# Feed-forward steps 3 to 10 with the gate and up products turned, and the down products placed one step sooner

## The chip, the cores and the metric

One core of one Trainium2 chip runs the whole kernel as a single launch. The metric is device time in microseconds (us). PE is the matrix engine (TensorE), PEld its weight loads, DVE the vector engine, ACT the scalar engine, POOL is GpSimd, SP the engine that issues the loads of weights.

## The reference

256 rows of width 1024 pass four transformer layers and then two layers of another kind. The change lies in the feed-forward part that closes each of the four:

```
def swiglu(x, w_gate_up, w_down):
    g, u = jnp.split(x @ w_gate_up, 2, axis=-1)
    return (jax.nn.silu(g) * u) @ w_down          # D_FF = 2816
x = layer_norm(ALPHA * x + swiglu(x, w_gate_up[i], w_down[i]), ln2_g[i], ln2_b[i])
```

The second kind of layer is conditioned by twelve rows of 512 values, `silu(c) @ w_ada + b_ada`. They depend on nothing else, and the kernel makes them in the midst of the feed-forward parts.

## The kernel before, in words

**Precision.** All is fp32. For a product the kernel splits each operand in a high part, rounded to the matrix engine's fp32r, and a low part, the rest, and adds three products: high by high, high by low, low by high. A tile of weights (128x2048, 1 MB) is loaded to one of three buffers `w_raw` (SP, line 2465), rounded to `w_high` by ACT (`high`, line 1528), and subtracted to `w_low` by DVE (`low`, line 1777). Five places hold high and low parts (`RING`). The loads of tile t wait until the low part of tile t-3 is made.

**Feed-forward.** `Plan.feed_forward` goes through 11 steps of 256 columns. A step has two tiles of `w_gate_up` (each half of the 1024 rows of the contraction, with 256 gate and 256 up columns) and one tile of `w_down`. I call the up tiles of step s sA and sB and its down tile Ds. Each tile is used by two jobs (`gemm`), one for each block of 128 rows of x (rb 0 and 1), each of 12 products of 512 columns. The rows' turned x (`xt_high`, `xt_low`) is the stationary operand, the weights move (line 1309). The result for 128 rows, gate in one half of a PSUM bank and up in the other, is read by ACT (`gate`: silu to SBUF, line 1663) and DVE (`gate`: times up, line 2128). Since the down product needs h with the hidden columns on the partitions, PE turns h of each step by four transposes (`turn_h`, line 1422), ACT copies them out as `ht_high` (line 1672), and DVE makes `ht_low` (line 2134). The down job (line 1268) has 12 products of 512 columns too and adds into PSUM banks kept for the whole layer. Steps 0 and 1 are made together, 3 to 9 are: up jobs A0, A1, B0, B1 of step s, a conditioning row if one is due, turn of h(s-1), then the two down jobs of D(s-3). Step 10 has no down. The tail does D7, D8, D9, D10 for rb 0, then for rb 1, with the turn of h(10) after D8.

**Conditioning rows.** After steps 3 to 8 a tile of `w_ada` is put in the stream (`ada_tile`). DVE multiplies and adds it (`ada_sum`, four instructions, line 1800) instead of splitting it. After every second tile the sum is split (lines 1679 and 2145), and two products by a matrix of ones (lines 1429, 1430) add over partitions. DVE adds the row to `ada_rows` (line 2154).

**Order.** Each engine runs the same list of steps, in order, and waits only on semaphores. When a tile has been used by both its jobs it is given back; `split()`, called after each job through `on()`, first emits the `low` of what was rounded at the split before, then, if a tile is owed, the next `high`, and only then counts what this job gave back. So tile n+5 is rounded one job after tile n was given back, and its low part is queued one job after that. Tiles are given back in order only: a tile used once holds back those behind it.

```
 def split(self):
     self.low()
     if self.owed:
         self.owed -= 1
         self.high()
     self.owed, self.given_back = self.owed + self.given_back, 0
```

**PSUM.** Banks 0 and 1 are the ring `gemms`, 6 and 7 the ring `tr` (for turns and conditioning rows). A use of a ring waits until the use two before it is released.

Of the kernel before, what the change touches and what calls it, by code (L numbers as in the profile page):

```python
# [50 lines left out]
RING = 5  # L51
PIECES = (4, 2)
N_TILES = (3 * KINDS.count("A") + len(KINDS) * (2 * (5 + 1 + 2) + 3 * FF_STEPS) + DEPTH_2 * 2 * (6 + 8 + 2))
BOTH = ("turned", "memory", "tail", "queries")
BESIDE = MEMW + IDX_H + HD
PAIRS = ((1, 2), (3, 0))
BIG = -1.0e30
# [93 lines left out]
class Plan:  # L151
# [127 lines left out]
    def block_turned(self, name, layer, cols, gen, then, begin=None):  # L279


        uses = [self.gemms.take() for _ in range(2)]
        for half in range(2):
            t = self.tile(name, layer, cols, "half", 4 * half)
            for n in range(2):
                self.gemm(t, n, half, gen, "gemm", uses[n], "turned")
                if half:
                    then(n, uses[n], t)
                if begin and half and n:
                    begin()  # L290
                self.on()

    def group(self, blocks, gen, after, prompt=False, more=None):
# [254 lines left out]
    def feed_forward(self, layer):  # L548

        gen, out = ("ff", layer), ("ln2", layer)  # L550
        acc = [self.wide.take() for _ in range(RB)]

        def gate(step):
            def then(rb, use, tile):
                self.up_use[layer, step, rb] = use
                self.add("gate", Ff(layer, step, rb, use, tile))
            return then

        def turn(step):
            self.ff_turn[layer, step] = self.tr.take()  # L560
            self.add("turn_h", (layer, step))

        def down(step, t, rb, prompt=False, part=None):
            self.gemm(t, rb, step, ("h", layer), "wide", acc[rb], "down", prompt, part)

        def down_tile(step):
            t = self.down_tile[layer, step] = self.tile("w_down", layer, step, "down", 0)
            return t

        def late():  # L570
            self.xt(gen, 1)
        self.group([("w_gate_up", layer, step, "up", gate(step)) for step in range(2)], gen,
                   [[self.split, self.split, late, self.split], [self.split] * 4])
        turn(0)
        for step in range(2, FF_STEPS):
            if step == 2:
                self.add("ada_ones", layer)
            self.block("w_gate_up", layer, step, gen, gate(step), "up")
            self.ada_row()
            if step == 2 and layer == LAST:  # L580
                self.add("load_modulation", 0)
            if step == 3 and layer in (1, LAST):
                self.add("norm_rows", layer // 2)
            if step == 9 and layer in (1, LAST):
                self.add("modulation", layer // 2)
            turn(step - 1)
            if step < FF_STEPS - 1:
                if step > 2:
                    t = down_tile(step - 3)
                    for rb in range(RB):  # L590
                        down(step - 3, t, rb)
                        self.on()
                if 2 < step < 9:
                    self.ada_tile()
        steps = range(FF_STEPS - 4, FF_STEPS)
# [576 lines left out]
def by_rows(j):  # L1172

    return j.kind == "dil"
# [37 lines left out]
def tensor_program(pe, K):  # L1212
# [29 lines left out]
    def idle(count):  # L1242

        pe.wait_ge(*K.zeroed.at(0))
        for _ in range(count):
            e.matmul(psum[:, K.wide.place(0), :], K.zeros[:, 0:P], K.zeros[:, :], start=True, stop=True)

    def gemm(j):
        s, rb = plan.place[j.tile] % RING, j.rb
        hi, lo = K.w_hi[:, s, :], K.w_lo[:, s, :]  # L1250
        if j.kind == "down":
            first, last = j.half == 0, j.half == FF_STEPS - 1
            if first:
# [3 lines left out]
            for n, h in passes:  # L1257
                if n == 0:
                    pe.wait_ge(*K.high.at(j.tile))
                    pe.wait_ge(*K.ht_high.at((j.gen[1], j.half)))  # L1260
                elif n == 1:
                    pe.wait_ge(*K.tr.out(plan.ff_turn[j.gen[1], j.half]))
# [243 lines left out]
def scalar_program(act, K):  # L1506
# [159 lines left out]
    def turn_h(j):  # L1666
        layer, step = j
        use = plan.ff_turn[j]
        if step > 3:
# [65 lines left out]
    def final_halves(_):  # L1735
# [6 lines left out]

    pieces = {"first_piece": first_piece, "high": high, "xt": xt, "rope_tables": rope_tables, "constants": constants, "evac": evac, "evac_ki": evac_ki,
              "turn": turn, "dots": dots, "exps": exps, "recip": recip, "turn_prob": turn_prob, "weigh": weigh, "mix_split": mix_split,
              "gate": gate, "turn_h": turn_h, "ada_halves": ada_halves, "rms": rms, "ret_weigh": ret_weigh, "sb_scores": sb_scores,
              "sb_halves": sb_halves, "sb_later": sb_later, "sb_split": sb_split, "final": final,
              "final_halves": final_halves}
    for what, job in plan.steps:
# [5 lines left out]
def vector_program(v, K):  # L1754
# [376 lines left out]
    def turn_h(j):  # L2131
# [2 lines left out]
        e.tensor_tensor(K.ht_lo[at], psum[:, K.tr.place(use), :].rearrange("p (c s) -> p c s", s=SEQ),  # L2134
                        K.ht_hi[at].bitcast(F32), ALU.subtract).then_inc(K.tr.sem(use), 1)

    def ada_ones(layer):
# [157 lines left out]
    def final(rb):  # L2297
# [9 lines left out]
              "turn_h": turn_h, "ada_ones": ada_ones, "ada_halves": ada_halves, "ada": ada, "modulation": modulation, "norm_rows": norm_rows, "rms": rms,  # L2307
# [166 lines left out]
class Kernel:  # L2474


    def __init__(self, nc, ctx, T, out):
# [16 lines left out]
        self.xt_hi = sb("xt_high", [P, KC, SEQ], F32R)  # L2494
        self.xt_lo = sb("xt_low", [P, KC, SEQ], F32R)
# [41 lines left out]
        self.ff_silu = [t.rearrange("p (r c) -> p r c", r=RB) for t in ff[0:2]]  # L2537
        self.ff_h = [t.rearrange("p (r c) -> p r c", r=RB) for t in ff[2:4]]
        self.ada_acc = ff[12:14]
        self.prob = [work[:, 1024 * n:1024 * n + 1024] for n in range(2)]  # L2540
        self.probt = [work[:, 2048 + 1024 * n:3072 + 1024 * n] for n in range(2)]
        self.idx = work[:, 2048:2048 + RB * 704].rearrange("p (r c) -> p r c", r=RB)
# [87 lines left out]
        self.silu_done, self.ht_high = signal("silu_done"), signal("ht_high")  # L2630
# [240 lines left out]
```

## Time and profile before

| | us |
|---|---|
| median of 3 runs (1553.69 to 1554.85) | 1554.36 |
| the profiled execution, its own time | 1553.68 |
| its span, first to last instruction | 1551.9 |
| PE busy | 1528.5 (98%) |
| DVE busy | 1088.2 (70%) |
| ACT busy | 760.7 (49%) |

The profiled execution took 1.8 us more than its span and 0.7 us less than the median. Busy times are sums over a whole engine; what one edit is worth is read in the stretch that it touches, from the starts of neighbouring instructions. In a row of the timeline "x4" is four instructions in a row, and the duration reaches from the start of the first to the end of the last; products overlap at their ends, so the pace is the distance between starts.

### The profile page before, as it was taken

The page shows a single profiled execution, that of the slowest core. Times are in us where ns is not written, and L with a number is a line of the kernel's source. Part 1 is how long each engine was busy: PE and PEld are TensorE (multiplying, and loading weights), DVE is VectorE, ACT ScalarE, POOL GpSimd, SP SyncE. Part 2 cuts the span into 40 slices and gives each one's busy share as a digit, 9 for nine tenths or more (in the row PEclk, how much of TensorE's full clock was granted, in tenths as well). Part 3 has the DMA queues.
Part 4 walks back from the last instruction along what each step waited for, and adds up shares of the span by engine and source line. Part 5 has one row for each costly group of instructions (what it writes and reads, how often), then busy time and mean ns, then how long its engine had stood idle before and what let it go on. Part 6 is the DMA issues. An engine that isn't in the chain of part 4 may idle for free.

```text
span 1551.9 us, 19840 instructions
## 1 busy us (share of the span) xinstructions
PE 1528.5 (98%) x8091; PEld 1267.8 (82%) x8091; DVE 1088.2 (70%) x1561; ACT 760.7 (49%) x963; POOL 52.1 (3%) x89
## 2 busy tenths in 40 slices
PE   9999999999999999999999999999999999999997
PEld 7887788888878888888788888877888888978986
DVE  6986866656777775676966756888667678567764
ACT  5657444444445443346544343566444434574463
POOL 1100000000000000000000000000100000000010
PEclk9999999999999999999999999999999999999999
DMA  8661666644435766352476654533766645433530
GB/s 320 245 231 55 226 224 264 249 174 179 163 104 201 262 261 243 138 215 83 178 252 234 244 225 148 204 109 136 267 257 236 223 166 223 164 118 140 217 122 27
DMA packets 45898, 299.87 MB, mean 193 GB/s; under 512 B 5540, under 2 KB 5796, under 8 KB 12528
## 3 DMA queue, kind: packets, MB, share of 16 engines
q1 hardware_dynamic: 39600, 278.74, 48.6%
q0 software_dynamic: 5776, 19.01, 3.7%
q8 instruction: 64, 1.05, 0.3%
q10 hardware_dynamic: 432, 0.85, 0.1%
q14 instruction: 26, 0.21, 0.0%
HBM read 296.20 MB, written 2.65 MB: 193 GB/s over the span
## 4 chain that ended last, share of the span: by engine, by line
PE 83%; DVE 9%; ACT 4%; issue 2%; DMA 0%; POOL 0%; POOLq 0%; SPq 0%; DVEq 0%; ACTq 0%
PE psum L1309 53%; PE psum L1268 15%; PE psum L1303 7%; DVE w_low L1777 3%; PE psum L1163 2%; PE psum L1238 1%; PE psum L1422 1%; ACT work L1604 1%; PE psum L1325 1%; ACT w_high L1528 1%; PE psum L1306 1%; DVE work L2061 1%; PE psum L1376 1%; DVE work L2099 1%; DVE xt_low L1811 0%
## 5 line engine op out<-in xcount | busy, mean ns | idle before, releaser
L1528 ACT ACTIVATE w_high<-w_raw 128x2048 fp32r<-128x2048 f32 (+1 forms) x240 | 456.4, 1903 | 230.7 <-DMA w_raw<-in_weights 144.9
L1777 DVE TENSOR_TENSOR w_low<-w_raw,w_high 128x2048 fp32r<-128x2048 f32 (+2 forms) x240 | 530.0, 2214 | 34.4 <-ACT w_high L1528 33.3
L1309 PE MATMUL psum<-w_high,xt_high 128*128 128x512 f32 (+1 forms) x1376 | 378.6, 395 | 1.4 <-DVE x_rows L1875 0.7
L1309 PE MATMUL psum<-w_high,xt_low 128*128 128x512 f32 (+1 forms) x1376 | 368.4, 388 | 0.3 <-DVE xt_low L1811 0.3
L1309 PE MATMUL psum<-w_low,xt_high 128*128 128x512 f32 (+1 forms) x1376 | 368.1, 388 | 0.0
L1309 PEld LDWEIGHTS psum<-w_high,xt_low 128*128 128x128 f32 x1376 | 257.4, 188 | 54.8 <-DVE xt_low L1811 0.7
L1309 PEld LDWEIGHTS psum<-w_low,xt_high 128*128 128x128 f32 x1376 | 257.3, 188 | 53.7 <-DVE w_low L1777 0.4
L1309 PEld LDWEIGHTS psum<-w_high,xt_high 128*128 128x128 f32 x1376 | 249.8, 188 | 52.5 <-DVE x_rows L1875 2.3
L2128 DVE TENSOR_TENSOR arena<-arena,psum 128x256 f32<-128x256 f32 x88 | 36.9, 420 | 205.4 <-ACT arena L1663 205.0
L1663 ACT ACTIVATE arena<-psum 128x256 f32<-128x256 f32 x88 | 33.7, 383 | 218.5 <-PE psum L1309 218.5
L1268 PE MATMUL psum<-w_high,ht_high 128*128 128x512 f32 x352 | 99.9, 401 | 0.0
L1268 PE MATMUL psum<-w_high,ht_low 128*128 128x512 f32 x352 | 96.1, 390 | 0.0
L1268 PE MATMUL psum<-w_low,ht_high 128*128 128x512 f32 x352 | 95.9, 390 | 0.0
L1268 PEld LDWEIGHTS psum<-w_high,ht_low 128*128 128x128 f32 x352 | 66.1, 188 | 14.4
L1268 PEld LDWEIGHTS psum<-w_low,ht_high 128*128 128x128 f32 x352 | 66.1, 188 | 14.1
L1268 PEld LDWEIGHTS psum<-w_high,ht_high 128*128 128x128 f32 x352 | 63.2, 188 | 11.0
L1560 ACT ACTIVATE arena<-psum 128x512 f32<-128x512 f32 (+1 forms) x54 | 30.4, 569 | 83.0 <-PE psum L1309 46.3
L1800 DVE SCALAR_TENSOR_TENSOR arena<-w_raw,c_col,arena 128x512 f32<-128x512 f32 x84 | 62.9, 749 | 2.6
L2364 POOL TENSOR_TENSOR norm_rstd<-norm_rstd,half_neg 128x1 f32<-128x1 f32 (+1 forms) x32 | 22.8, 715 | 1126.8 <-DVE norm_rstd L1860 871.2
L1604 ACT ACTIVATE work<-work,neg_max 128x128 f32<-128x128 f32 (+3 forms) x80 | 38.0, 477 | 28.2 <-DVE neg_max L2061 27.9
L1920 DVE TENSOR_SCALAR arena<-psum 128x512 f32<-128x512 f32 x25 | 17.2, 688 | 48.3 <-PE psum L1309 25.4
L1811 DVE TENSOR_TENSOR xt_low<-psum,xt_high 128x512 fp32r<-128x512 f32 (+1 forms) x48 | 31.0, 672 | 18.0 <-ACT xt_high L1537 17.5
(253 smaller groups left out, 1494.8 us busy)
## 6 DMA issues: line engine op xcount, KB each, us to landing
w_raw<-in_weights SPq DMA_DIRECT2D x260, 1024.0 KB, 4.8
norm_params<-in_ln_g POOLq DMA_DIRECT2D x8, 512.0 KB, 4.4
norm_params<-in_ln_b POOLq DMA_DIRECT2D x8, 512.0 KB, 5.9
w_raw<-in_weights SPq DMA_DIRECT2D x4, 656.0 KB, 6.1
kv_outside<-arena POOLq DMA_DIRECT2D x3, 512.0 KB, 4.5
mem_kv<-kv_outside POOLq DMA_DIRECT2D x3, 512.0 KB, 3.7
norm_params<-mods_outside POOLq DMA_DIRECT2D x3, 512.0 KB, 5.8
x_rows<-in_x SPq DMA_DIRECT2D x4, 256.0 KB, 5.6
```

Of the source, the lines that this page charges most:

```text
L1163: m = e.matmul(pieces[n][1], left, right, start=banks[i] not in banks[:i], stop=banks[i] not in banks[i + 1:])
L1268: m = e.matmul(psum[:, K.wide.place(j.use) + h, :], left[:, c, rb * P:rb * P + P], right[:, w:w + BLK], start=first and c == 0 and n == 0, ...
L1303: m = e.matmul(dst, right[:, c + b * P:c + b * P + P], rows[:, kk, :], start=first and b == 0, stop=last and b == 1)
L1309: m = e.matmul(psum[:, bank, 0:w], rows[:, kk, rb * P:rb * P + P], right[:, at:at + w], start=first, stop=last)
L1528: e.activation(K.w_hi[:, g % RING, 0:w], K.w_raw[:, r, 0:w], ACT.Copy).then_inc(K.high.hit(t), 1)
L1560: m = e.activation(to, out, ACT.Silu if j.silu else ACT.Copy, scale=K.evac_scale(j.where, j.rb))
L1604: m = e.activation(pr, pr, ACT.Exp, bias=K.negmax[:, slot, n:n + 1], scale=-1.0, accum_out=K.expsum[:, slot, n:n + 1])
L1663: e.activation(K.ff_silu[j.step % 2][:, j.rb, :], psum[:, K.gemms.place(j.use), 0:FF_STEP], ACT.Silu).then_inc(K.silu_done.hit((j.layer, j ...
L1777: m = e.tensor_tensor(K.w_lo[:, s, 0:n], K.w_raw[:, r, 0:n], K.w_hi[:, s, 0:n].bitcast(F32), ALU.subtract)
L1800: m = e.scalar_tensor_tensor(out=acc, in0=w, scalar=c, in1=acc, op0=ALU.mult, op1=ALU.add)
L1811: m = e.tensor_tensor(lo[at], psum[:, K.tr.place(j.use), 0:n * P].rearrange("p (c s) -> p c s", s=P), hi[at].bitcast(F32), ALU.subtract)
L2128: e.tensor_tensor(K.ff_h[j.step % 2][:, j.rb, :], K.ff_silu[j.step % 2][:, j.rb, :], bank[:, FF_STEP:BLK], ALU.mult).then_inc(K.gemms.sem( ...
```

## The change

- From step 3 (`BY_ROWS`) on, up jobs are made the other way about (`block_up`, `gemm_up`). The weights are stationary, 128 columns at a time, and the rows' high and low parts, laid out as one buffer `xt_both`, move together. A job n takes the columns n*128 to n*128+127 of gate and of up: eight products of 512 columns (256 rows by high part, 256 by low) and eight of 256 columns with the low weights. h comes out with the hidden columns on the partitions. Job 0 takes both banks of `gemms`, job 1 both of `tr`.
- The half of each bank that holds weights by the rows' low parts is copied out by ACT (`gate_turned`, 128x512) and added to the other half by DVE, gate and up apart. Then come ACT's silu and DVE's product. The wait for ACT's silu stands behind the DVE's first addition.
- The transposes of `turn_h` go for steps 3 to 10. `split_h` on ACT and DVE makes `ht_high` and `ht_low` from SBUF. Steps 0 to 2 keep theirs.
- Down jobs move: step s has D(s-2) and not D(s-3), beginning with D0 in step 2. Step 8 has D6 for rb 0 alone, step 9 D6 for rb 1 alone, step 10 none, and the tail is as it was, with `split_h` of step 10 after D8. The turn of h(2) stands between the two jobs of D0.
- The conditioning row stands after a down job and not ahead of the turn. The `modulation` of step 9 follows the down job.

```
@@ Plan @@
+    def block_up(self, layer, step, gen):
+        uses = [(ring.take(), ring.take()) for ring in (self.gemms, self.tr)]
+        for half in range(2):
+            t = self.tile("w_gate_up", layer, step, "up", 4 * half)
+            for n in range(2):
+                self.gemm(t, n, half, gen, ("gemm", "turn")[n], uses[n], "up")
+                if half:
+                    self.add("gate_turned", Up(layer, step, n, uses[n], t))
+                self.on()
@@ feed_forward @@
         def turn(step):
-            self.ff_turn[layer, step] = self.tr.take()
-            self.add("turn_h", (layer, step))
+            if step < BY_ROWS:
+                self.ff_turn[layer, step] = self.tr.take()
+                self.add("turn_h", (layer, step))
+            else:
+                self.add("split_h", (layer, step))
...
-            self.block("w_gate_up", layer, step, gen, gate(step), "up")
-            self.ada_row()
+                self.block("w_gate_up", layer, step, gen, gate(step), "up")
+            else:
+                self.block_up(layer, step, gen)
...
-            turn(step - 1)
-            if step < FF_STEPS - 1:
-                if step > 2:
-                    t = down_tile(step - 3)
-                    for rb in range(RB):
-                        down(step - 3, t, rb)
-                        self.on()
-                if 2 < step < 9:
-                    self.ada_tile()
+            if step != BY_ROWS:
+                turn(step - 1)
+            if step == FF_STEPS - 1:
+                break
+            if step < FF_STEPS - 2:
+                t = down_tile(step - 2)
+            for rb in range(RB) if step < FF_STEPS - 3 else (step - FF_STEPS + 3,):
+                down(min(step - 2, FF_STEPS - 5), t, rb)
+                self.on()
+                self.ada_row()
+                if rb == 0 and step == BY_ROWS - 1:
+                    turn(step)
...
+            if 2 < step < 9:
+                self.ada_tile()
@@ tensor_program @@
+    def gemm_up(j, hi, lo):
...
+        work = [(4 * j.half + k, b, k * BLK + b * FF_STEP + j.rb * P) for k in range(4) for b in range(2)]
+        pe.wait_ge(*K.high.at(j.tile))
+        for kk, b, c in work:
+            e.matmul(banks[b].rearrange("p (n s) -> p n s", n=2), hi[:, c:c + P], K.xt_both[:, :, kk, :], start=kk == 0, stop=False)
+        pe.wait_ge(*K.taken.at(j.tile))
+        for kk, b, c in work:
+            m = e.matmul(banks[b][:, 0:SEQ], lo[:, c:c + P], K.xt_both[:, 0, kk, :], start=False, stop=kk == KC - 1)
@@ scalar_program @@
+    def gate_turned(j):
...
+        e.activation(K.ff_rest[j.n], psum[:, first:first + 2, SEQ:BLK], ACT.Copy).then_inc(K.rest_out.hit((j.layer, j.step, j.n)), 1)
+        act.wait_ge(*ring.out(j.uses[0]))
+        e.activation(K.ff_silu[j.step % 2][:, j.n, :], K.ff_gate(j), ACT.Silu).then_inc(K.silu_done.hit((j.layer, j.step, j.n)), 1)
@@ vector_program @@
+    def gate_turned(j):
...
+        for use, row in zip(j.uses, (K.ff_gate(j), K.ff_up(j))):
+            e.tensor_tensor(row, psum[:, ring.place(use), 0:SEQ], row, ALU.add).then_inc(ring.sem(use), 1)
...
+        e.tensor_tensor(K.ff_h[j.step % 2][:, j.n, :], K.ff_silu[j.step % 2][:, j.n, :], K.ff_up(j),
+                        ALU.mult).then_inc(K.h_made.hit((j.layer, j.step, j.n)), 1)
+    def split_h(j):
...
+        v.wait_ge(*K.ht_high.at(j))
+        e.tensor_tensor(K.ht_lo[at], K.ff_h[j[1] % 2], K.ht_hi[at].bitcast(F32),
+                        ALU.subtract).then_inc(K.ht_low.hit(j), 1)
```

## Rows read from the trace of the kernel before

**Rows 1.** The page, parts 1 and 2: busy us, share, instructions; granted clock in tenths

```profile
PE 1528.5 (98%) x8091; PEld 1267.8 (82%) x8091; DVE 1088.2 (70%) x1561; ACT 760.7 (49%) x963; POOL 52.1 (3%) x89
...
PEclk9999999999999999999999999999999999999999
```

**Rows 2.** The waits of PE: us in total, times, longest us

```profile
PE psum L1376 <- ACT arena L1648: 2.3, 3, 1.2
...
PE psum L1238 <- DVE arena L2117: 1.7, 1, 1.7
```

**Rows 3.** Busy time by stretch, a step without a conditioning row and one with

```profile
230.23:247.05 16.82, 16.82 (x78) 13.90 (x76) 11.13 (x12) 7.42 (x7) 0.00 (x0) 1.00 0.67 251
247.05:264.29 17.24, 17.24 (x79) 14.28 (x78) 11.95 (x12) 6.90 (x6) 0.00 (x0) 1.00 0.68 255
```

**Rows 4.** The timeline of the second of these: start us, duration us, instruction

```profile
252.49 1.07 PE L1309 MATMUL psum<-w_high,xt_high 128*128 128x512 f32 x4
...
255.21 1.07 PE L1309 MATMUL psum<-w_high,xt_high 128*128 128x512 f32 x4
...
257.93 0.39 PE L1429 MATMUL psum<-ada_high,ones 128*128 128x512 f32 x1
...
258.38 0.60 PE L1422 MATMUL psum<-ident,arena 128*128 128x128 f32 x4
...
258.88 2.28 DVE L1777 TENSOR_TENSOR w_low<-w_raw,w_high 128x2048 fp32r<-128x2048 f32 x1
...
262.35 3.09 DVE L1800 SCALAR_TENSOR_TENSOR arena<-w_raw,c_col,arena 128x512 f32<-128x512 f32 x4
...
264.29 1.07 PE L1309 MATMUL psum<-w_high,xt_high 128*128 128x512 f32 x4
...
265.85 1.92 ACT L1528 ACTIVATE w_high<-w_raw 128x2048 fp32r<-128x2048 f32 x1 [4.42 <-DMA w_raw<-in_weights]
```

**Rows 5.** The timeline of a stretch of products of 256 columns

```profile
1331.62 1.12 PE L1303 MATMUL psum<-xt_high,w_high 128*128 128x256 f32 x8
1332.58 1.12 PE L1303 MATMUL psum<-xt_low,w_high 128*128 128x256 f32 x8
```

**Rows 6.** The timeline of steps 9, 10 and the tail of layer 0

```profile
332.67 1.92 ACT L1528 ACTIVATE w_high<-w_raw 128x2048 fp32r<-128x2048 f32 x1 [3.13 <-PE psum L1268]
...
341.05 1.91 ACT L1528 ACTIVATE w_high<-w_raw 128x2048 fp32r<-128x2048 f32 x1
...
343.30 0.60 PE L1422 MATMUL psum<-ident,arena 128*128 128x128 f32 x4
343.50 0.38 ACT L1663 ACTIVATE arena<-psum 128x256 f32<-128x256 f32 x1 [0.53 <-PE psum L1309]
343.65 1.18 PE L1268 MATMUL psum<-w_high,ht_high 128*128 128x512 f32 x4
343.92 0.42 DVE L2128 TENSOR_TENSOR arena<-arena,psum 128x256 f32<-128x256 f32 x1 [2.30 <-ACT arena L1663]
343.93 0.60 ACT L1672 ACTIVATE ht_high<-psum 128x512 fp32r<-128x512 f32 x1
344.25 2.29 DVE L1777 TENSOR_TENSOR w_low<-w_raw,w_high 128x2048 fp32r<-128x2048 f32 x1
344.43 1.91 ACT L1528 ACTIVATE w_high<-w_raw 128x2048 fp32r<-128x2048 f32 x1
...
346.45 0.68 DVE L2134 TENSOR_TENSOR ht_low<-psum,ht_high 128x512 fp32r<-128x512 f32 x1
...
347.06 2.28 DVE L1777 TENSOR_TENSOR w_low<-w_raw,w_high 128x2048 fp32r<-128x2048 f32 x1
```

**Rows 7.** DMA issues of the weights: KB each, us to landing

```profile
w_raw<-in_weights SPq DMA_DIRECT2D x260, 1024.0 KB, 4.8
```

**Rows 8.** The page, part 5: the weight loads of the down products, mean ns

```profile
L1268 PEld LDWEIGHTS psum<-w_high,ht_low 128*128 128x128 f32 x352 | 66.1, 188 | 14.4
```

**Rows 9.** The timeline of PE at the kernel's start, products on zeros

```profile
1.19 3.17 PE L1246 MATMUL psum<-arena 128*128 128x512 bf16 x7 [1.19 <-DVE arena L1757]
```

More of the change, by code:

```diff
@@ L39 @@
 FF_STEPS = D_FF // FF_STEP
+BY_ROWS = 3
 ALPHA = float((2 * len(KINDS)) ** 0.25)
@@ L53 @@
 N_TILES = (3 * KINDS.count("A") + len(KINDS) * (2 * (5 + 1 + 2) + 3 * FF_STEPS) + DEPTH_2 * 2 * (6 + 8 + 2))
-BOTH = ("turned", "memory", "tail", "queries")
+BOTH = ("turned", "memory", "tail", "queries", "up")
 BESIDE = MEMW + IDX_H + HD
@@ L145 @@
 Ff = namedtuple("Ff", "layer step rb use tile")
+Up = namedtuple("Up", "layer step n uses tile")
 Ada = namedtuple("Ada", "row use")
@@ L1246, in idle @@
             e.matmul(psum[:, K.wide.place(0), :], K.zeros[:, 0:P], K.zeros[:, :], start=True, stop=True)
+    def gemm_up(j, hi, lo):
+        ring = (K.gemms, K.tr)[j.rb]
+        if j.half == 0:
+            for use in j.use:
+                pe.wait_ge(*ring.free(use))
+        banks = [psum[:, ring.place(use), :] for use in j.use]
+        for r in range(RB):
+            use = plan.xt_uses[j.gen, r, j.half]
+            pe.wait_ge(*K.xt_high.at(use))
+            pe.wait_ge(*K.tr.out(use))
+        work = [(4 * j.half + k, b, k * BLK + b * FF_STEP + j.rb * P) for k in range(4) for b in range(2)]
[5 more added lines that the diff above has]
+            m = e.matmul(banks[b][:, 0:SEQ], lo[:, c:c + P], K.xt_both[:, 0, kk, :], start=False, stop=kk == KC - 1)
+        m.then_inc(K.multiplied.hit((j.tile, j.rb)), 1)
     def gemm(j):
@@ L1250, in gemm @@
         hi, lo = K.w_hi[:, s, :], K.w_lo[:, s, :]
+        if j.kind == "up":
+            gemm_up(j, hi, lo)
+            return
         if j.kind == "down":
@@ L1261, in gemm @@
                 elif n == 1:
-                    pe.wait_ge(*K.tr.out(plan.ff_turn[j.gen[1], j.half]))
+                    pe.wait_ge(*(K.tr.out(plan.ff_turn[j.gen[1], j.half]) if j.half < BY_ROWS
+                                 else K.ht_low.at((j.gen[1], j.half))))
                 else:
@@ L1673, in turn_h @@
                      ACT.Copy).then_inc(K.ht_high.hit(j), 1)
+    def gate_turned(j):
+        ring = (K.gemms, K.tr)[j.n]
+        first = min(ring.place(use) for use in j.uses)
+        act.wait_ge(*K.multiplied.at((j.tile, j.n)))
+        if j.step > BY_ROWS:
+            act.wait_ge(*K.h_made.at((j.layer, j.step - 1, j.n)))
+        e.activation(K.ff_rest[j.n], psum[:, first:first + 2, SEQ:BLK], ACT.Copy).then_inc(K.rest_out.hit((j.layer, j.step, j.n)), 1)
+        act.wait_ge(*ring.out(j.uses[0]))
+        e.activation(K.ff_silu[j.step % 2][:, j.n, :], K.ff_gate(j), ACT.Silu).then_inc(K.silu_done.hit((j.layer, j.step, j.n)), 1)
+    def split_h(j):
+        layer, step = j
+        if step > 3:
+            act.wait_ge(*K.multiplied.at((plan.down_tile[layer, step - 4], 1)))
+        for n in range(2):
+            act.wait_ge(*K.h_made.at((layer, step, n)))
+        e.activation(K.ht_hi[step % 4], K.ff_h[step % 2], ACT.Copy).then_inc(K.ht_high.hit(j), 1)
     def ada_halves(row):
@@ L1744, in scalar_program @@
               "turn": turn, "dots": dots, "exps": exps, "recip": recip, "turn_prob": turn_prob, "weigh": weigh, "mix_split": mix_split,
-              "gate": gate, "turn_h": turn_h, "ada_halves": ada_halves, "rms": rms, "ret_weigh": ret_weigh, "sb_scores": sb_scores,
+              "gate": gate, "turn_h": turn_h, "gate_turned": gate_turned, "split_h": split_h, "ada_halves": ada_halves, "rms": rms, "ret_weigh": ret_weigh, "sb_scores": sb_scores,
               "sb_halves": sb_halves, "sb_later": sb_later, "sb_split": sb_split, "final": final,
@@ L2135, in turn_h, with split_h @@
                         K.ht_hi[at].bitcast(F32), ALU.subtract).then_inc(K.tr.sem(use), 1)
+    def gate_turned(j):
+        ring = (K.gemms, K.tr)[j.n]
+        v.wait_ge(*K.rest_out.at((j.layer, j.step, j.n)))
+        for use, row in zip(j.uses, (K.ff_gate(j), K.ff_up(j))):
+            e.tensor_tensor(row, psum[:, ring.place(use), 0:SEQ], row, ALU.add).then_inc(ring.sem(use), 1)
+        if j.step - 2 < BY_ROWS:
+            v.wait_ge(*K.turned.at(plan.ff_turn[j.layer, j.step - 2]))
+        else:
+            v.wait_ge(*K.ht_low.at((j.layer, j.step - 2)))
+        v.wait_ge(*ring.out(j.uses[1]))
+        v.wait_ge(*K.silu_done.at((j.layer, j.step, j.n)))
+        e.tensor_tensor(K.ff_h[j.step % 2][:, j.n, :], K.ff_silu[j.step % 2][:, j.n, :], K.ff_up(j),
+                        ALU.mult).then_inc(K.h_made.hit((j.layer, j.step, j.n)), 1)
+    def split_h(j):
+        at = j[1] % 4
+        v.wait_ge(*K.ht_high.at(j))
+        e.tensor_tensor(K.ht_lo[at], K.ff_h[j[1] % 2], K.ht_hi[at].bitcast(F32),
+                        ALU.subtract).then_inc(K.ht_low.hit(j), 1)
     def ada_ones(layer):
@@ L2306, in vector_program @@
               "choose": choose, "scores": scores, "recip": recip, "turn_prob": turn_prob, "weigh": weigh, "mix_split": mix_split, "gate": gate,
-              "turn_h": turn_h, "ada_ones": ada_ones, "ada_halves": ada_halves, "ada": ada, "modulation": modulation, "norm_rows": norm_rows, "rms": rms,
+              "turn_h": turn_h, "gate_turned": gate_turned, "split_h": split_h, "ada_ones": ada_ones, "ada_halves": ada_halves, "ada": ada, "modulation": modulation, "norm_rows": norm_rows, "rms": rms,
               "modulate": modulate, "rotate": rotate, "ret_scores": ret_scores, "ret_norm": ret_norm,
@@ L2493, in __init__ @@
         self.w_lo = sb("w_low", [P, RING, TW], F32R)
-        self.xt_hi = sb("xt_high", [P, KC, SEQ], F32R)
-        self.xt_lo = sb("xt_low", [P, KC, SEQ], F32R)
+        self.xt_both = sb("xt_both", [P, 2, KC, SEQ], F32R)
+        self.xt_hi, self.xt_lo = self.xt_both[:, 0, :, :], self.xt_both[:, 1, :, :]
         self.x = sb("x_rows", [P, RB, D])
@@ L2539, in __init__ @@
         self.ada_acc = ff[12:14]
+        self.ff_rest = [work[:, BLK * n:BLK * n + BLK].rearrange("p (b s) -> p b s", b=2) for n in range(2)]
         self.prob = [work[:, 1024 * n:1024 * n + 1024] for n in range(2)]
@@ L2735, in group_on_scalar, with ff_gate, ff_up @@
         return 0 if by_rows(j) and self.unit_pieces(j) > 4 else None
+    def ff_gate(self, j):
+        places = [(self.gemms, self.tr)[j.n].place(use) for use in j.uses]
+        return self.ff_rest[j.n][:, int(places[0] > places[1]), :]
+    def ff_up(self, j):
+        places = [(self.gemms, self.tr)[j.n].place(use) for use in j.uses]
+        return self.ff_rest[j.n][:, int(places[0] < places[1]), :]
     def unit_pieces(self, j):
```

3 lines of the change are left out of this document (2 added, 1 removed).

## The prediction

> **What bounds the kernel now.** I read the page first: PE is busy 98% of the span, DVE 70%, ACT 49%, at the full granted clock in all slices [rows 1]. So what counts is PE's own instructions, and any new wait of PE. PE's waits come next: the largest group is 2.3 us in all, the longest single one 1.7 us, and no line of the feed-forward (L1309 up, L1268 down, L1422 turn) has one worth naming [rows 2]. The stretches confirm it: a step of 16.82 us and one of 17.24 us are PE busy from end to end, with DVE busy 11.13 and 11.95 us and ACT 7.42 and 6.90 us [rows 3]. The timeline gives the parts. Three groups of four products start 2.72 us apart for a job of 12: 0.2267 us for one of 512 columns [rows 4]. The conditioning row takes 257.93 to 258.38, 0.45 us; from there to the next step's first product are 5.91 us, of which two down jobs are 24 x 0.2267 = 5.44, so the turn of h costs PE 0.47 us [rows 4]. The step of rows 3 without a row gives 16.82 - 72 x 0.2267 = 0.50. I take 0.48.
>
> **Removed.** 8 turns x 4 layers = 32 x 0.48 = 15.4 us, all on PE, which sets the time.
>
> **Added on PE.** A job has now 8 products of 512 and 8 of 256 columns: the same 6144 columns, four instructions more. 256 columns go at 0.96 / 8 = 0.120 us [rows 5]. The job is 8 x 0.2267 + 8 x 0.120 = 2.77 us against 2.72, and 128 jobs (4 x 8 x 4) cost 128 x 0.053 = +6.8 us. Those 256-column rows have weights as the moving side; the pace should hang on columns alone. That the 512 columns now come from two places 256 apart in xt_both has no row: I take nothing, bounded by nothing and by the pace of two products of 256 (0.240 for 0.227, 1024 products: +13.7 us), and lean to nothing, since both ends are runs of 256 neighbours. Solved for two widths, rows 4 and 5 give 0.0133 us per product beyond 2.4 GHz streaming.
> The Trainium skill (TensorE: Matmul & The Clock Gate, "Wait — 56ns, not 53.3ns?") has only about 2.5 ns per warm product on top of N/2.4 GHz. By that this term would be 512 x 2.5 ns = 1.3 us and not 6.8. The trace's 13 ns disagrees, and it decides.
>
> **Added on ACT and DVE, hidden in steps 3 to 9.** Per step: ACT two copies of 128x512 (0.60 each) more, DVE four additions of 128x256 for the banks (starts 0.33 apart, 343.92 to 344.25) [rows 6] and the wait for silu. I walk a step with a row from t = 0, the end of B0; queue starts from rows 6: PE end to ACT 0.20, ACT end to DVE 0.04, silu to the next 0.28, a low part 2.20 to the next, a subtraction of 512 0.61.
> - Job 0: copy 0.20-0.80, additions 0.84 and 1.17, silu 1.31, product 1.73-2.06. ACT then rounds a tile 1.59-3.50.
> - Job 1 (PE ends 2.77): copy 3.5-4.1, additions 4.15 and 4.5, product 5.1-5.4. Then on DVE low 5.4-7.6, split of h 8.2, ada_sum (3.09 [rows 4]) 11.3, row or its split 12.0, low 14.2, low 16.4. The next step's first addition is due at 17.0 + 0.84 = 17.8: 1.4 us to spare.
> - PE's conditioning row wants job 1's first bank at 5.49, it is free at 4.6: 0.9 us to spare. The next up jobs want the banks 8.2 us after their last product.
> - The loads: ACT already sits 4.42 us before 265.85 for a tile that waits for the low part of 258.88 [rows 4]. That low part comes 1.7 us later, so the rounding ends near 14.2 instead of 12.6, still 3 us ahead of the next copy of B0.
> Price: 0. Where a spare falls under zero, PE waits once a step (rival 2).
> The moves in steps 2 to 9 cost nothing either: D(s-2) reads a split of h one step old; the turn of h(2) has a down job of 2.72 us over the gate chain, 0.6 us now (343.30 to 343.92 and on). SP's loads keep their number and only change order; POOL gets no new instruction.
>
> **Added in the tail.** This is the term that decides. D6 is used once in step 8 and once after step 9, and tiles come back in order. So 9A and 9B wait behind it, nothing is rounded in step 9, and D7, D8, D9, D10 are rounded in the four jobs of step 10, the next layer's first tile N in the job after. In the kernel before D9 starts at 332.67 on the end of D6, D10 at 341.05, N at 344.43, and N's low part at 347.06 lies ahead of the tail's second job [rows 6]. Now, from t = 0 at the end of 10B0 (D7 and D8 rounded by then, D7 low too; D8's low is queued behind job 0's DVE work):
> - DVE: additions 0.84, 1.17; product 1.73; low D8 2.06-4.35; job 1's additions 4.26, 4.59 (its copy ran 3.4-4.0 behind the rounding of D9), product 5.15, low D9 5.48, split of h(9) 7.68, low D10 8.29-10.5.
> - N's load waits for low D8, is issued at 4.35 and lands 4.8 us later [rows 7], 9.15. ACT rounds N 9.15-11.06 and then, behind it, copies h(10) 11.1-11.7. DVE: low N 11.1, split of h(10) 13.3-13.98.
> - PE: 10B1 ends 2.77, D7, D8, D9 at 10.93. D10 wants the high part of h(10) at 10.93 and gets it at 11.7; after two products, 0.45, its pass by the low part was due at 11.38, but stands till 14.0.
> So D10 of rb 0 ends 2.6 us late. After each of the two stops a weight load (0.188 [rows 8]) lies bare that was covered; I add 0.2. If N's load did not hold, DVE alone (low N at 10.49, split 12.69-13.37) would still give 2.0. Bounds 1.9 to 3.2, taken 2.8, in four layers: +11.2 us (7.6 to 12.8). Nothing behind takes it back, as PE is busy from the tail on; the later loads (N+1 lands near 12.6, wanted after D7 of rb 1) are in time.
>
> **Sum.** -15.4 + 6.8 + 11.2 = +2.6 us. Against the profiled execution's 1553.68: 1556.3. The median lies 0.7 above that execution, so the median becomes 1557.0. A measurement tells about 0.2%, 3.1 us, from no change; the forecast lies just within it.
>
> **Rivals.**
> 1. The tail does not stall: N's low part or the split of h(10) comes earlier than I walk, or the tiles are given back otherwise. For it: the tail before has no PE wait at all. Against: even the DVE queue alone is 2 us too long. Time: -15.4 + 6.8 = -8.6, 1545.8. Chance 0.20.
> 2. Slower, by DVE in the steps with a w_ada tile. Place: the DVE queue from gate_turned of job 0 to the last low of the step, the scalar waits for DVE's first addition standing in it. Spare 1.4 us of 17; it decides where the queue takes over 1.4 us more than walked, or, for the rows, where job 1's first addition slips by 0.9. Against: all durations in it have rows. For: two engines hand over four times a job, with an in-order rounding between them. At 0.3 us a step over 6 x 4 steps: +7, 1564. Chance 0.15.
> 3. PE's clock falls in the new gap of 2 us. Before, the longest wait was 1.7 us at full granted clock [rows 1, 2], so nothing shows a fall. The nearest row of slow products is the start, 7 of 512 columns in 3.17 us, 0.45 each, about twice rows 4's pace [rows 9]. Such a stretch in each tail, of which half is lost: 4 x 1.6 = +6, 1563. Chance 0.03.
> 4. The four extra instructions of a job cost little, as the skill's figure has it, and the walk is right in the rest. From rows, a job of the same columns at the 512 pace would cost 2.72: the 6.8 falls away, 1550.2. Chance 0.05.
>
> **How the numbers follow.** The forecast has 0.57. Its own range is 1553.5 to 1560 (tail 7.6 to 12.8, turn cost 0.47 to 0.50, moving operand up to +2). It splits at 1557.5: 0.37 within 0.2%, 0.20 above. Faster: rivals 1 and 4, 0.25. Slower: 0.20 + rival 2 + rival 3, 0.38. Same: 0.37. The range must take in rival 1's 1545.8, and reaches up to 1562, leaving out the upper end of rival 2, rival 3 and a dearer operand: some 0.15.
>
> **What would show it.** Right: no L1422 after step 2; up jobs of 2.77 us; steps without a row 16.5 us, PE busy throughout; in each tail one or two PE waits of together 2 to 3 us before D10 of rb 0, ended by DVE's split of h(10), with ACT idle on the load of N just before. Wrong: a tail with PE busy throughout (rival 1); PE waits at the conditioning rows or up jobs of steps 5, 7, 9 (rival 2); a granted clock under 1.00 behind the tail's gap (rival 3); products of 512 columns from xt_both spaced by more or less than 0.227 us, or a job of 2.72.

## The result, and the profile after

The changed kernel takes 1568.62 us (median; 1567.33 to 1569.49) against 1554.52 for the kernel before: ratio 1.0093, 95% interval 1.0081 to 1.0105, +14.1 us. 1557.0 was forecast, in a range that ended at 1562, so the prediction is wrong. The profiled executions, on which the accounts below rest, are 15.8 us apart (1569.49 and 1553.68). The profiled one of the changed kernel is the slowest of its four and has the lowest mean granted clock, 0.996; the fastest (1567.33) has 0.998.

The page of the changed kernel, beside rows 1: PE's busy time hardly moved, so the loss is in waits and slow stretches. The row of the clock is made of nines, as before, and yet the clock fell three times, as shown below: a slice is 39 us long, and a digit 9 says 90% or more.

```profile
PE 1530.0 (98%) x8475; PEld 1284.5 (82%) x8475; DVE 1137.5 (73%) x1689; ACT 797.3 (51%) x1027; POOL 52.8 (3%) x89
...
PEclk9999999999999999999999999999999999999999
```

The waits of PE in the changed kernel (us in total, times, longest), beside rows 2:

```profile
PE psum L1315 <- DVE ht_low L2219: 6.5, 4, 1.6
PE psum L1285 <- DVE ada_rows L2239: 4.7, 8, 0.9
PE psum L1315 <- ACT ht_high L1738: 3.0, 4, 0.8
PE psum L1423 <- ACT arena L1695: 2.3, 3, 1.2
```

L1315 is the down product, L1285 the turned up product with the high weights, L1288 the one with the low weights. The first and third rows are the tail's waits that the prediction walked. The second was not foreseen. The timeline shows where it stands:

```profile
268.51 3.11 DVE L1865 SCALAR_TENSOR_TENSOR arena<-w_raw,c_col,arena 128x512 f32<-128x512 f32 x4
269.07 1.98 PE L1285 MATMUL psum<-xt_both,w_high 128*128 128x512 f32 x8
270.88 1.11 PE L1288 MATMUL psum<-xt_both,w_low 128*128 128x256 f32 x8
271.66 0.74 DVE L2239 SCALAR_TENSOR_TENSOR ada_rows<-psum,ident,ada_rows 12x512 f32<-12x512 f32 x1
...
272.54 2.08 PE L1285 MATMUL psum<-xt_both,w_high 128*128 128x512 f32 x8 [0.55 <-DVE ada_rows L2239]
...
275.41 2.00 PE L1285 MATMUL psum<-xt_both,w_high 128*128 128x512 f32 x8
277.25 1.12 PE L1288 MATMUL psum<-xt_both,w_low 128*128 128x256 f32 x8
278.20 2.00 PE L1285 MATMUL psum<-xt_both,w_high 128*128 128x512 f32 x8
```

The row's two products sit in a `tr` bank that the second up job of the next step needs. DVE reads the row (L2239) only after the four instructions of ada_sum (L1865), 3.1 us. This happens in steps 6 and 8 of each layer. The last three lines give the job's length, 278.20 - 275.41 = 2.79 us.

The tail of layer 0 answers to rows 6. D7 starts at 343.68, N's load holds ACT until 350.20, and D10 of rb 0 stops twice:

```profile
343.06 2.28 DVE L1842 TENSOR_TENSOR w_low<-w_raw,w_high 128x2048 fp32r<-128x2048 f32 x1
...
350.20 1.92 ACT L1575 ACTIVATE w_high<-w_raw 128x2048 fp32r<-128x2048 f32 x1 [1.74 <-DMA w_raw<-in_weights]
...
352.78 0.70 PE L1315 MATMUL psum<-w_high,ht_high 128*128 128x512 f32 x2 [0.76 <-ACT ht_high L1738]
...
354.36 0.68 DVE L2219 TENSOR_TENSOR ht_low<-arena,ht_high 128x512 fp32r<-128x512 f32 x1
...
355.10 0.73 PE L1315 MATMUL psum<-w_high,ht_low 128*128 128x512 f32 x2 [1.62 <-DVE ht_low L2219]
```

The stretches around the stop, in layer 0 and in layer 3 (busy us by engine, then granted clock, DMA share, GB/s):

```profile
352.00:355.00 3.00, 0.73 (x3) 0.30 (x2) 2.85 (x2) 0.64 (x2) 0.00 (x0) 1.00 1.01 382
355.00:356.00 1.00, 0.90 (x4) 0.74 (x5) 0.04 (x1) 0.00 (x0) 0.00 (x0) 0.93 1.00 360
356.00:359.00 3.00, 3.00 (x9) 2.32 (x8) 1.38 (x2) 0.00 (x0) 0.00 (x0) 0.50 0.83 339
...
1270.00:1273.00 3.00, 0.97 (x3) 0.56 (x4) 2.68 (x2) 0.27 (x1) 0.00 (x0) 1.00 1.00 377
1273.00:1276.00 3.00, 3.00 (x14) 2.47 (x14) 2.01 (x3) 0.00 (x0) 0.00 (x0) 1.00 0.99 396
```

PE worked 0.73 of the 3 us from 352 to 355, and behind that the clock was at 0.50, the 1.2 GHz level: 9 instructions in 3 us where layer 3, after the same two stops, ran 14. The clock fell in layers 0, 1 and 2 of this execution, not in layer 3.

**Where 15.8 us came from**, by the starts of PE's blocks in both traces (a block is the four up jobs of a step):
- turns away: 32 x 0.48 = -15.4;
- up blocks 11.15 us instead of 10.89, 32 times: +8.3;
- the up blocks of steps 6 and 8, eight in all, 11.91 to 12.29 instead of 11.15: +6.5;
- tails. Layer 0, from D7 to the next layer's first product: 370.91 - 343.68 = 27.23, before 366.91 - 343.30 = 23.61 less two turns of 0.48 = 22.65, so +4.6. Layers 1 to 3: +4.5, +4.6, +3.0. Together +16.7, of which the fallen clock has 3 x 1.6.

The ends of layer 0's tail, before and after:

```profile
366.91 1.07 PE L1309 MATMUL psum<-w_high,xt_high 128*128 128x512 f32 x4
...
370.91 1.98 PE L1356 MATMUL psum<-w_high,xt_both 128*128 128x512 f32 x8
```

The sum is +16.1, which leaves 0.3 unexplained.

### The profile page after: what moved, and what is told of

Read it like the earlier page. It is cut to its first block, busy times and chain, and to the rows that moved or that the text cites. A ratio compares the mean times of both kernels' runs of the same rounds, so it can differ in the third digit from the quotient of the medians.

```text
span 1567.7 us, 20859 instructions
## 1 busy us (share of the span) xinstructions
PE 1530.0 (98%) x8475; PEld 1284.5 (82%) x8475; DVE 1137.5 (73%) x1689; ACT 797.3 (51%) x1027; POOL 52.8 (3%) x89
## 4 chain that ended last, share of the span: by engine, by line
PE 73%; DVE 15%; ACT 7%; issue 3%; DMA 2%; SPq 0%; POOL 0%; POOLq 0%; DVEq 0%; ACTq 0%
PE psum L1356 30%; PE psum L1285 12%; PE psum L1315 10%; PE psum L1350 7%; PE psum L1288 6%; DVE w_low L1842 5%; ACT w_high L1575 3%; DMA w_raw<-in_weights 2%; PE psum L1186 2%; DVE arena L1865 2%; PE psum L1261 1%; ACT work L1651 1%; PE psum L1372 1%; ACT work L1728 1%; PE psum L1353 1%
## 5 line engine op out<-in xcount | busy, mean ns | idle before, releaser
L1356 PE MATMUL psum<-w_high,xt_both 128*128 128x512 f32 (+1 forms) x1728 | 435.9, 393 | 1.8 <-DVE x_rows L1940 0.8
L1356 PEld LDWEIGHTS psum<-w_high,xt_both 128*128 128x128 f32 x1728 | 315.0, 188 | 67.2 <-DVE x_rows L1940 2.3
L1285 PE MATMUL psum<-xt_both,w_high 128*128 128x512 f32 x1024 | 256.1, 392 | 4.7 <-DVE ada_rows L2239 4.7
L1356 PE MATMUL psum<-w_low,xt_both 128*128 128x512 f32 (+1 forms) x864 | 231.1, 387 | 0.0
L1285 PEld LDWEIGHTS psum<-xt_both,w_high 128*128 128x128 f32 x1024 | 186.1, 188 | 40.7 <-issue 6.1
L1356 PEld LDWEIGHTS psum<-w_low,xt_both 128*128 128x128 f32 x864 | 161.2, 188 | 33.9 <-DVE w_low L1828 0.6
L1288 PEld LDWEIGHTS psum<-xt_both,w_low 128*128 128x128 f32 x1024 | 139.7, 190 | 10.0
L1288 PE MATMUL psum<-xt_both,w_low 128*128 128x256 f32 x1024 | 142.7, 282 | 0.0
L2206 DVE TENSOR_TENSOR work<-psum,work 128x256 f32<-128x256 f32 x128 | 48.3, 419 | 117.2 <-ACT work L1728 117.2
L1315 PE MATMUL psum<-w_high,ht_low 128*128 128x512 f32 x352 | 98.3, 397 | 6.5 <-DVE ht_low L2219 6.5
L1315 PE MATMUL psum<-w_high,ht_high 128*128 128x512 f32 x352 | 99.6, 400 | 3.0 <-ACT ht_high L1738 3.0
L1315 PE MATMUL psum<-w_low,ht_high 128*128 128x512 f32 x352 | 97.7, 395 | 0.0
L1315 PEld LDWEIGHTS psum<-w_high,ht_low 128*128 128x128 f32 x352 | 66.7, 190 | 22.5 <-DVE ht_low L2219 8.2
L1315 PEld LDWEIGHTS psum<-w_low,ht_high 128*128 128x128 f32 x352 | 67.5, 192 | 14.4
L1315 PEld LDWEIGHTS psum<-w_high,ht_high 128*128 128x128 f32 x352 | 64.1, 192 | 15.6 <-ACT w_high L1575 4.6
L1350 PE MATMUL psum<-xt_both,w_high 128*128 128x256 f32 x512 | 67.8, 285 | 0.0
L1865 DVE SCALAR_TENSOR_TENSOR arena<-w_raw,c_col,arena 128x512 f32<-128x512 f32 x84 | 62.9, 748 | 2.6
L1350 PEld LDWEIGHTS psum<-xt_both,w_high 128*128 128x128 f32 x512 | 63.7, 191 | 0.3
```

Source lines behind the costliest of these rows:

```text
L1285: e.matmul(banks[b].rearrange("p (n s) -> p n s", n=2), hi[:, c:c + P], K.xt_both[:, :, kk, :], start=kk == 0, stop=False)
L1288: m = e.matmul(banks[b][:, 0:SEQ], lo[:, c:c + P], K.xt_both[:, 0, kk, :], start=False, stop=kk == KC - 1)
L1315: m = e.matmul(psum[:, K.wide.place(j.use) + h, :], left[:, c, rb * P:rb * P + P], right[:, w:w + BLK], start=first and c == 0 and n == 0, ...
L1350: m = e.matmul(dst, right[:, c + b * P:c + b * P + P], rows[:, kk, :], start=first and b == 0, stop=last and b == 1)
L1356: m = e.matmul(psum[:, bank, 0:w], rows[:, kk, rb * P:rb * P + P], right[:, at:at + w], start=first, stop=last)
L1865: m = e.scalar_tensor_tensor(out=acc, in0=w, scalar=c, in1=acc, op0=ALU.mult, op1=ALU.add)
```

## The experiments

Each run is compared with the kernel before on the same chip (1553.6 to 1555.0 there).

**D6 whole.** Tests whether the held-back tiles make the tail wait.

```
-            if step < FF_STEPS - 2:
-                t = down_tile(step - 2)
-            for rb in range(RB) if step < FF_STEPS - 3 else (step - FF_STEPS + 3,):
+            if step != FF_STEPS - 3:
+                t = down_tile(min(step - 2, FF_STEPS - 5))
+            for rb in range(RB) if step != FF_STEPS - 3 else ():
```

> The changed kernel, with both jobs of D6 in step 9 and none in step 8 (nothing is held back). Theory A, the tail waits because D6 used once keeps 9A and 9B from being given back: D7 and D8 are rounded in step 9 again, PE waits for neither half of h(10), the clock stays at 1.00 in all four tails. The four tails cost 16.6 us more than before now (4.6 in layers 0 to 2, 3.0 in layer 3), so the time falls by 15 to 17 us, to about 1552. Theory B, the heavier gate work of step 10 on ACT and DVE is too long for the tail by itself: a wait of over 1 us stays in each tail, and the time stays above 1560.

Measured: 1553.00 us, ratio 0.9991 (0.9981 to 1.0000), 15.6 below the changed kernel. Of the feed-forward's waits of PE one row is left, and the tails have none:

```profile
PE psum L1285 <- DVE ada_rows L2239: 3.0, 4, 1.4
```

Theory A holds: with D6 whole the tails of layers 0 to 2 take 22.68 us, where the kernel before less its two turns has 22.65, so the tile used once made all the tails' loss, the clock's share included. The roundings show why. The changed kernel's ACT rounds nothing for 12 us before 332.33 (first line); here it rounds at 326.44 and 330.15 too, and N at 347.22 without a wait for its load:

```profile
332.33 3.72 ACT L1575 ACTIVATE w_high<-w_raw 128x2048 fp32r<-128x2048 f32 x2 [0.78 <-PE psum L1315]
...
326.44 1.90 ACT L1575 ACTIVATE w_high<-w_raw 128x2048 fp32r<-128x2048 f32 x1
330.15 1.90 ACT L1575 ACTIVATE w_high<-w_raw 128x2048 fp32r<-128x2048 f32 x1
...
347.22 1.90 ACT L1575 ACTIVATE w_high<-w_raw 128x2048 fp32r<-128x2048 f32 x1
```

**Row read first.** Tests what held the bank.

```
-                self.on()
                 self.ada_row()
+                self.on()
```

> The changed kernel, with ada_row ahead of on() after a down job, so that DVE adds the conditioning row before the ada_sum of the next w_ada tile; PE's order is the same. Theory A, the second up job after a row waits since its PSUM bank is held behind that ada_sum (3.1 us): the eight waits of 0.55 to 0.90 go, and with each the slow restart; 8 x 0.78 + 0.35 = 6.6 us less, about 1562. Theory B, DVE has too much to do in these steps: the wait goes to another place (first addition late, or a low part late), time within 2 us of 1568.6.

Measured: 1560.19 us, ratio 1.0038 (1.0023 to 1.0053), 8.4 below. No wait on L2239 is left. In its timeline DVE reads the row ahead of the ada_sum, and the second up job starts 2.77 us after the first, without a wait:

```profile
269.22 0.73 DVE L2239 SCALAR_TENSOR_TENSOR ada_rows<-psum,ident,ada_rows 12x512 f32<-12x512 f32 x1
...
269.78 1.98 PE L1285 MATMUL psum<-xt_both,w_high 128*128 128x512 f32 x8
269.88 3.10 DVE L1865 SCALAR_TENSOR_TENSOR arena<-w_raw,c_col,arena 128x512 f32<-128x512 f32 x4
...
272.55 2.00 PE L1285 MATMUL psum<-xt_both,w_high 128*128 128x512 f32 x8
```

Theory A again; DVE had time enough, in the wrong order. The 8.4 us are more than the 6.6 expected. In this run's profile the clock fell in two tails (layers 0 and 3), not three, which is worth 1.6. The granted clocks of the four executions agree, 0.997 to 0.999 against 0.996 to 0.998. The tails' waits are the same as before (L1315: 6.5 and 2.9 us), so this part is put down to chance and not to the edit; no run tests that.

**Filler in the gap.** Tests the clock alone: the path waits for the same things. `FILL` picks a bank of `gemms` that nobody uses then.

```
                 elif n == 1:
+                    if last and rb == 0 and h == 0 and j.part is None:
+                        use = FILL(plan, j)
+                        pe.wait_ge(*K.gemms.out(use))
+                        for _ in range(8):
+                            e.matmul(psum[:, K.gemms.place(use), :], K.ht_hi[j.half % 4][:, 0, 0:P], hi[:, 0:BLK], start=True, stop=True)
```

> The changed kernel, with eight more products of 512 columns (1.8 us) into a free PSUM bank in each tail, between the first pass of D10 of rb 0 and its pass with the low part of h(10), where PE stands idle now. Nothing is waited for less. Theory A, PE's idle gap lets the clock fall: it stays at 1.00 in the tails, products behind the gap come 0.227 us apart and not 0.427, and 3 x 1.6 = 4.8 us go: about 1564. Theory B, the clock falls for another reason or the filler pushes the path: no gain, or up to 1 us a tail more.

Measured: 1565.37 us, ratio 1.0072 (1.0057 to 1.0088), 3.2 below; the profiled executions differ by 4.5. The same stop, filled (L1316 is the filler):

```profile
353.38 0.70 PE L1324 MATMUL psum<-w_high,ht_high 128*128 128x512 f32 x2 [0.72 <-ACT ht_high L1747]
353.91 2.02 PE L1316 MATMUL psum<-w_high,ht_high 128*128 128x512 f32 x8
355.77 0.67 PE L1324 MATMUL psum<-w_high,ht_low 128*128 128x512 f32 x2
356.27 0.62 PE L1324 MATMUL psum<-w_low,ht_high 128*128 128x512 f32 x2
```

And the stretch behind it, in its table of stretches (columns as above):

```profile
356.00:359.00 3.00, 3.00 (x14) 2.44 (x13) 2.03 (x3) 0.00 (x0) 0.00 (x0) 1.00 0.92 374
```

The pass with the low part starts 2.39 us after the first pass, in the changed kernel 2.32, so the wait is as long as before. The clock stays at 1.00 in all four tails, where it fell in five of the eight tails of the changed kernel and of the run above, with this stop unfilled. Thirty-two useless products, eight in each tail, buy 3 to 4.5 us: the clock's fall hangs on the gap. What decides whether it comes behind a given stop, no run shows.

**The moves alone**, with the up jobs of the kernel before.

```
-BY_ROWS = 3
+BY_ROWS = 11
...
+            if step < BY_ROWS:
                 self.block("w_gate_up", layer, step, gen, gate(step), "up")
...
-                if rb == 0 and step == BY_ROWS - 1:
+                if rb == 0 and step == 2 and BY_ROWS == 3:
```

> The changed kernel with BY_ROWS = 11: the up jobs, gates and turns of the kernel before, but the down jobs and conditioning rows where the change puts them (D6 split over steps 8 and 9; the turn of h(2) stands after step 3 and not between the jobs of D0). Theory A, the tail's wait needs both the held-back tiles and the gate work: DVE's queue is about 1.8 us shorter here, N's low part ends near 12.3 us after 10B0, and PE with two turns in its path wants the low part of h(10) at 12.3: a wait of 0.3 to 1.2 us in a tail, clock at 1.00, time 1555.5 to 1559. Theory B, the split of D6 is enough by itself: waits over 2 us in a tail, clock falls in some, 1564 to 1570. Theory C, downs one step sooner gain something: under 1553.

Measured: 1556.92 us, ratio 1.0017 (1.0008 to 1.0027), +2.4. In its tails PE waits once, and nowhere else in the feed-forward:

```profile
PE psum L1316 <- DVE ht_low L2200: 2.0, 4, 0.6
```

Theory A: the split of D6 costs 0.6 us a layer by itself; with the gates' DVE work queued among the late roundings it costs 2.4 us of waits and 0.6 of slow restarts, and then the clock. The places of the down jobs bring nothing to the up jobs of old: the 2.4 us are the tails' four times 0.6.

**Both mends.** The edits of the first two runs together.

> The changed kernel with both mends: both jobs of D6 in step 9, and ada_row ahead of on(). Theory A: what is left of the change is the turn's 15.4 us against jobs of 2.79 us (128 x 0.067 = 8.6 us dearer). The wait of the second up job after a row (four of 0.5 to 1.4 us in the run with D6 whole) goes; a wait of about 0.3 us may stay at the row of step 7. Time 1547.5 to 1550. Theory B, the two mends hang on the same thing and don't add: 1552 to 1554.

Measured: 1548.51 us, ratio 0.9964 (0.9952 to 0.9976): 5.1 us below the kernel before and 20.1 below the changed one (19.2 if each is set against the kernel before on its own chip). This version beats both. The down job ahead of step 7's row and the row take 3.57 us (300.87 - 297.30) instead of 3.20. The row waits until DVE's additions (L2206), queued behind an ada_sum, have read its bank, so 0.37 us a layer is still lost there:

```profile
297.30 1.09 PE L1315 MATMUL psum<-w_high,ht_high 128*128 128x512 f32 x4
...
299.83 0.76 DVE L2206 TENSOR_TENSOR work<-psum,work 128x256 f32<-128x256 f32 x2
...
300.31 0.50 PE L1476 MATMUL psum<-ada_high,ones 128*128 128x512 f32 x1
...
300.87 1.09 PE L1315 MATMUL psum<-w_high,ht_high 128*128 128x512 f32 x4
```

**Parts laid side by side**, on top of both mends.

```
-        self.xt_both = sb("xt_both", [P, 2, KC, SEQ], F32R)
+        self.xt_both = sb("xt_both", [P, KC, 2, SEQ], F32R)
...
-                e.matmul(..., K.xt_both[:, :, kk, :], ...)
+                e.matmul(..., K.xt_both[:, kk, :, :], ...)
```

> As the run with both mends, and the rows' high and low parts lie next to each other for each 128 of the contraction (xt_both [128, 8, 2, 256]), so that a product of 512 columns reads one run of 512. Theory A, the pace of 0.230 us of these products against 0.227 of others comes from the two runs of 256: 0.227, the up block of a step 11.04 us in place of 11.15, 1024 x 0.0034 = 3.5 us less than the run with both mends. Theory B, it comes from the switch between products of 512 and 256 columns or from weights as the stationary side: the pace stays 0.230 and the time within 1 us.

Measured: 1550.19 us, ratio 0.9972 (0.9961 to 0.9983). The times of both runs lie in two clusters, 1548.2 to 1548.9 and 1550.1 to 1550.5, and the fastest of each is 1548.25; the medians differ by which cluster has more. The granted clock of the executions is 0.999 (one 0.998) in the lower cluster and 0.997 or 0.998 in the upper, and the profiled two show a reason. The one of both mends (1550.38) has a fall of the clock near 1283 us, at the start of the fifth layer, far from what the mends change; this run's (1548.29) has the same waits there and no fall. So the medians' 1.7 us go with the clock and not with the layout. The pace did not move either:

```profile
235.56 1.98 PE L1285 MATMUL psum<-xt_both,w_high 128*128 128x512 f32 x8
237.37 1.12 PE L1288 MATMUL psum<-xt_both,w_low 128*128 128x256 f32 x8
238.33 2.00 PE L1285 MATMUL psum<-xt_both,w_high 128*128 128x512 f32 x8
240.17 1.11 PE L1288 MATMUL psum<-xt_both,w_low 128*128 128x256 f32 x8
```

Theory A falls. Eight products of 512 take 1.81 us (237.37 - 235.56) when others of 512 stand before them, and 1.84 (240.17 - 238.33) behind products of 256. That switch comes at three of a block's four jobs. Both groups have weights as the stationary side, so of Theory B's two causes it is the switch.

**The downs at their old places**, with turned up jobs and the row read first.

```
-            if step != BY_ROWS:
-                turn(step - 1)
+            turn(step - 1)
...
-            for rb in range(RB) if step < FF_STEPS - 3 else (step - FF_STEPS + 3,):
-                down(min(step - 2, FF_STEPS - 5), t, rb)
+            for rb in range(RB) if step > 2 else ():
+                down(step - 3, t, rb)
```

> Turned up products with the down jobs where the kernel before has them (D0 to D6 in steps 3 to 9, both jobs each, D(s-3)), the turn of h(2) right behind the up jobs of step 3, and ada_row ahead of on(). Theory A, placing the downs one step sooner pays only by hiding that turn: its four transposes want a PSUM bank that the second job of step 3 has just filled, so PE waits 1.2 to 2 us there in each layer, nothing else changes, and the time is 5 to 8 us above the run with both mends (1548.5): 1553.5 to 1556.5. Theory B, the sooner place has no worth of its own: no wait there, 1548 to 1550. Theory C, h of a step comes too late or tiles run short somewhere else: over 1558.

Measured: 1566.33 us, ratio 1.0071 (1.0054 to 1.0088): 17.8 above both mends (16.5 if each is set against the kernel before on its own chip). The time is in Theory C's range, but neither of its two causes is what the trace shows. Layer 0 in its timeline (L1282 up, L1466 the turn):

```profile
216.19 0.42 DVE L2190 TENSOR_TENSOR arena<-arena,psum 128x256 f32<-128x256 f32 x1 [0.57 <-ACT arena L1707]
...
216.71 3.12 PE L1282 MATMUL psum<-xt_both,w_high 128*128 128x512 f32 x8 [1.82 <-issue]
...
231.21 0.66 PE L1466 MATMUL psum<-ident,arena 128*128 128x128 f32 x4 [1.55 <-DVE work L2203]
```

The stretch behind the first wait of PE, in its table of stretches (columns as above):

```profile
217.00:220.00 3.00, 3.00 (x10) 2.42 (x9) 3.00 (x3) 1.91 (x1) 0.00 (x0) 0.58 0.96 352
```

The wait of Theory A is there (231.21, 1.55 us). It had missed another: without D0 in step 2, the first turned job needs both `gemms` banks right behind step 2's last job and one turn, and DVE (L2190) has read the second of them only at 216.61. PE idles 1.8 us (up to 2.6 in other layers), and the clock falls there in layers 0 to 2 (0.58 above). From the turn of h(0) to the next layer's first product layer 0 takes 169.1 us against 164.2 in the run with both mends, 4.9 more; layers 1 to 3 take 5.8, 5.0 and 3.5 more. So with this ring of banks the turned products pay only if D0 stands in step 2; without it they lose more than they save.

## Why the prediction was wrong, point by point

- **"What bounds the kernel now"** was right: every us below is PE's.
- **"Removed", 15.4 us**: right as far as the sum closes to 0.3.
- **"Added on PE", +6.8**: measured +8.3. The 0.0133 us a product held (a block of 11.09 was expected); the 0.03 at each return from 256 to 512 columns, seen in no row before, makes the rest. The prediction's estimate from the Trainium skill (TensorE: Matmul & The Clock Gate, "Wait — 56ns, not 53.3ns?"), with its 2.5 ns a product, was 1.3, farther off. Rival 4 falls with it: a job takes 2.79 us and not 2.72.
- **"The next up jobs want the banks 8.2 us after their last product" is the step that failed first.** The ring `tr` has two banks. The second up job takes both, and behind a row one of them was used last by the row and not by an up job. That bank is free when DVE has read the row, walked in the very list at 12.0 us; the job wants it at 8.65 (the earlier job, two down jobs and the row) + 2.79 (the job ahead of it) = 11.4. The numbers to find the 0.6 us stood there and were not set against each other. In the trace it is 0.55 to 0.90, with the restart 0.8 on average, eight times: +6.5, priced at 0. Rival 2 looked for such waits at the rows and at the up jobs of steps 5, 7 and 9, by DVE's running over its 17 us. They stand at the up jobs of steps 6 and 8, and DVE did not run over: the other order of the same work takes them away (1560.19 us).
- **"Added in the tail", 2.8 a layer**: 3.0 in layer 3, where the clock held. From the end of 10B0 (340.88), low D8 ended at 4.46 us (walked 4.35), ACT began N at 9.32 (9.15), h(10)'s last split began at 13.48 (13.3), PE went on at 14.22 (14.0). Rival 1 did not come: the stop is in all four tails.
- **Rival 3, the clock, at 0.03**, was the second failure. It came true on top of the forecast: 1.6 us in each of three tails, +4.8 (I gave it 1.6 in each of four, +6). The forecast took it for unlikely because no trace showed a fall; the longest PE wait before was 1.7 us, and the new stop has 0.76 and 1.62 us with 0.70 us of work between them. A row that shows nothing beyond 1.7 us speaks for neither side there, and it deserved a large chance. The nines of rows 1 could not have shown a fall at all. In the kernel before the clock did hold, but one trace says little: the fifth layer starts with waits of about 1.07 and 0.73 us in every run here. The granted clock is 1.00 behind them in the kernel before (first two lines, columns as above) and 0.52 in the run with D6 whole (last line):

```profile
1287.64 0.66 PE L1238 MATMUL psum<-ident,work 128*128 128x128 f32 x4 [0.73 <-DVE work L2185]
...
1288.00:1291.00 3.00, 3.00 (x16) 2.50 (x15) 2.27 (x5) 0.60 (x1) 2.18 (x4) 1.00 0.48 162
...
1288.00:1291.00 3.00, 3.00 (x10) 2.35 (x9) 2.27 (x5) 0.60 (x1) 2.16 (x4) 0.52 0.51 160
```

- **Sum.** The forecast's 2.6 + 6.5 (rows) + 4.8 (clock) + 1.5 (jobs) + 0.7 (tails) = 16.1.
- **The range** had the rows' wait and the clock as one rival each, never both with the forecast's own stall. (By the prediction's own terms it runs from 1552.8 to 1560.9, not 1553.5 to 1560; that changes nothing here.)

## What to carry to other kernels

When a change makes an operation take a bank from a ring that others share, list the ring's uses in order and put each user's release beside the next taker's need, the small users (a row, a turn) too; the late one is a reader queued behind something long, and moving it ahead of that costs nothing (swapping two lines gave some 4 us on top of the run with D6 whole, and 8.4 on the changed kernel, where the clock also happened to fall less often). A tile half used holds back everything behind it in an in-order ring; look for its price not where it stands but where the roundings bunch up. A new idle gap of PE can cost more than its length: behind the stall of some 2.4 us here the clock fell in five of eight tails, some 1.6 us each time, and an estimate should carry that at its chance. A full clock in one trace, or in the tenths of a page, is weak evidence that it will not.

## What the runs showed of the hardware

- After stops of 0.6 to 0.8 and 1.6 us with two products between them the granted clock was 0.50 for 3 to 4 us in three of four tails of the changed kernel and in two of four with the row read first, and stayed 1.00 in the others. Eight useless products in the gap kept it at 1.00 in all four.
- Behind waits of 1.07 and 0.73 us at the start of the fifth layer it fell in two of nine profiled executions (D6 whole, both mends) and held in the kernel before.
- A product of 512 columns with a moving operand in two runs of 256 goes at the same pace as with one run (1.81 us for eight, both ways).
- Return from products of 256 to products of 512 columns: 0.03 us for the group (1.84 against 1.81).
